# Swapping the two halves of the memory projection, and where the residual's norm runs

## The reference, cut to what matters

```python
x = x + mix @ w_out[l]

h = rms_norm(x, norm_x[l])            # "n2" in the kernel
m = rms_norm(mem, norm_mem[l])        # "nm", 256 tokens
q = (h @ xq[l]).reshape(B, S, XATTN_HEADS, XATTN_DH)
k, v = jnp.split(m @ xkv[l], 2, axis=-1)
...
q = rms_norm(q, xq_gain[l])
k = rms_norm(k, xk_gain[l])
s = jnp.einsum('bshd,bmhd->bhsm', q, k).astype(jnp.float32) * (XATTN_DH ** -0.5)
p = jax.nn.softmax(s, axis=-1).astype(v.dtype)
o = jnp.einsum('bhsm,bmhd->bshd', p, v).reshape(B, S, D)
x = x + o @ xo[l]
```

## Time and profile before

| | |
|---|---|
| median of 3 runs | 2663.01 us (2656.39 to 2664.89) |
| the profiled execution | 2657.79 us |
| its span in the trace | 2656.0 us |
| TensorE busy | 2451.6 us, 92% |
| VectorE, ScalarE, GpSimd busy | 989.9, 861.7, 841.8 us |
| mean granted clock of TensorE | 0.964 |

### The profile page before, as it was taken

The page is one execution under the profiler, slowest core; times in us unless marked ns, Lnnn a source line. Parts: engine busy times, 40 slices in busy tenths (PEclk is TensorE's granted clock), DMA queues, the critical chain, the costliest instruction groups (busy, mean ns, idle before and its releaser), DMA issues.

```text
span 2656.0 us, 33639 instructions
## 1 busy us (share of the span) xinstructions
PE 2451.6 (92%) x12246; PEld 1970.2 (74%) x12246; DVE 989.9 (37%) x1483; ACT 861.7 (32%) x1215; POOL 841.8 (32%) x347
## 2 busy tenths in 40 slices
PE   6989988887999997999999996999989998999997
PEld 4767567665878775888888883977766876678885
DVE  3231443148978787121111126034214443421114
ACT  3233344343422225221211223145433533432222
POOL 2222125303444443332222232232222023344442
PEclk9999789998999998999999998999999999999998
DMA  4112023223555552122221221222222012123322
GB/s 137 63 55 79 17 64 112 90 78 125 190 191 190 179 184 68 56 66 64 63 64 56 63 79 46 64 70 92 64 69 71 1 48 79 63 95 95 96 94 94
DMA packets 66563, 230.72 MB, mean 87 GB/s; under 512 B 7216, under 2 KB 9520, under 8 KB 66352
## 3 DMA queue, kind: packets, MB, share of 16 engines
q1 hardware_dynamic: 50224, 179.36, 21.1%
q10 hardware_dynamic: 16256, 50.21, 5.8%
HBM read 226.66 MB, written 2.10 MB: 86 GB/s over the span
## 4 chain that ended last, share of the span: by engine, by line
PE 50%; issue 37%; POOL 8%; DVE 4%; ACT 1%; DMA 1%; POOLq 0%; DVEq 0%; ACTq 0%; SPq 0%
PE ps L1258 35%; PE ps L1276 12%; POOL WLO L287 7%; DVE TN L1062 1%; DVE DOT L966 1%; PE ps L1470 1%; DVE TN L782 0%; DMA RAW<-in_stream_dram 0%; PE ps L1451 0%; PE ps L1317 0%; DMA CB<-in_c_dram 0%; PE ps L1360 0%; PE ps L1291 0%; ACT SQ L346 0%; DVE X L860 0%
## 5 line engine op out<-in xcount | busy, mean ns | idle before, releaser
L287 POOL TENSOR_TENSOR WLO<-RAW,WHI 128x1024 fp32r<-128x1024 f32 x335 | 829.6, 2481 | 1770.5 <-ACT WHI L314 1770.4
L314 ACT ACTIVATE WHI<-RAW 128x1024 fp32r<-128x1024 f32 x335 | 354.8, 1059 | 862.3 <-DMA RAW<-in_stream_dram 763.1
L1258 PE MATMUL ps<-HLO,WHI 128*128 128x512 f32 (+1 forms) x1312 | 438.6, 369 | 18.2 <-DVE OLO L835 5.2
L1258 PE MATMUL ps<-HHI,WLO 128*128 128x512 f32 (+1 forms) x1312 | 430.8, 363 | 1.9 <-issue 1.9
L1258 PE MATMUL ps<-HHI,WHI 128*128 128x512 f32 (+1 forms) x1312 | 430.6, 363 | 0.0
L1258 PEld LDWEIGHTS ps<-HLO,WHI 128*128 128x128 f32 x1312 | 227.9, 189 | 67.2 <-issue 25.2
L1276 PE MATMUL ps<-HHI,WHI 128*128 128x512 f32 (+1 forms) x640 | 223.4, 382 | 42.5 <-DVE HLO L1040 17.5
L1258 PEld LDWEIGHTS ps<-HHI,WHI 128*128 128x128 f32 x1312 | 227.9, 189 | 41.6 <-issue 2.9
L1258 PEld LDWEIGHTS ps<-HHI,WLO 128*128 128x128 f32 x1312 | 228.0, 189 | 39.3
L1258 PE MATMUL ps<-GLO,WHI 128*128 128x512 f32 x704 | 229.4, 366 | 16.8 <-DVE GLO L989 8.4
L984 DVE TENSOR_TENSOR SF<-SF,ps 128x512 f32<-128x512 f32 (+1 forms) x66 | 51.2, 777 | 490.4 <-PE ps L1258 368.5
(11 more groups left out here) (289 smaller groups left out, 3312.7 us busy)
## 6 DMA issues: line engine op xcount, KB each, us to landing
RAW<-in_stream_dram SPq DMA_DIRECT2D x335, 512.0 KB, 3.6
ADA<-in_ada_dram ACTq DMA_DIRECT2D x72, 512.0 KB, 3.9
BM<-in_bias_dram ACTq DMA_DIRECT2D x8, 448.0 KB, 3.8
DECAY<-in_decay_dram ACTq DMA_DIRECT2D x4, 512.0 KB, 3.7
out_dram<-X SPq DMA_DIRECT2D x8, 256.0 KB, 2.0
X<-in_x_dram SPq DMA_DIRECT2D x2, 512.0 KB, 5.8
X<-in_x_dram ACTq DMA_DIRECT2D x2, 512.0 KB, 7.6
C<-in_mem_dram ACTq DMA_DIRECT2D x1, 1024.0 KB, 5.4
```

The source lines that it names most:

```text
L287: nc.gpsimd.tensor_tensor(WLO[:, slot(u)], RAW[:, slot(u)], WHI[:, slot(u)].bitcast(F32), ALU.subtract).then_inc(unit_lo, 1)
L314: nc.scalar.activation(WHI[:, j], RAW[:, j], ACT.Copy).then_inc(unit_hi, 1)
L1258: mm = nc.tensor.matmul(out, w, x[:, k, tok], start=(k == 0 and n == 0), stop=(k == kt - 1 and n == 2))
```

## The change

The values come before the keys: in the stream of weights, on TensorE, on ScalarE and on VectorE. "n2" moves ahead of the keys on ScalarE and VectorE. Its sum over partitions stands on TensorE behind the first pair of values. On TensorE the wait for all eight residual tiles becomes a wait for the tile whose bank a pair of values takes. The converts inside "n2" are shifted by one: unit `xv`+3 is converted ahead of the norm, then one unit behind each of the first seven roundings. TensorE's wait for `xv` now stands ahead of the keys and its wait for `xk_q` ahead of the queries.

```diff
-... ("w_out", 8), ("xk", 8), ("xv", 8), ("xq", 8),
+... ("w_out", 8), ("xv", 8), ("xk", 8), ("xq", 8),
...
             act.wait_ge(*norm_at("n2", "acc", KD + 1))
+            convert(UNIT["xv"] + AHEAD)
+            norm("n2", None, KD, S, D, RS, SQ, TN, dst=HHI,
+                 between=lambda k: convert(UNIT["xv"] + AHEAD + k + 1) if k < 7 else None)
             normed("xk", UNIT["xk"], 2, 2, M, 256, SQ, RS)
-            act.wait_ge(s("xk_q"), 8)
-            norm("n2", None, KD, S, D, RS, SQ, TN, dst=HHI, between=lambda k: convert(UNIT["xv"] + AHEAD + k))
             normed("xq", UNIT["xq"], 2, 2, S, 256, SQ, RS)
...
-            normed("xk", UNIT["xk"], 2, 2, M, RS, ...)
             dve.wait_ge(s("w_out_x"), KD + 4)
             dve.wait_ge(*norm_at("nm", "lo", KD))
             norm("n2", lambda k: X[:, k], KD, S, lambda k: col("norm_x", k), RS, TN, HHI, HLO)
             for a in range(4):
                 wait_unit(UNIT["xv"] + 2 * a + 1)
                 V.tensor_copy(XV[:, :, 256 * a:256 * a + 256], ...).then_inc(s("xv"), 1)
+            normed("xk", UNIT["xk"], 2, 2, M, RS, ...)
...
-            pe.wait_ge(s("w_out_x"), KD + 4)
-            normed("xk", UNIT["xk"], 2, 2, M, const[:, ONES], SQ, (HHI, HLO), slice(S, N2))
-            sum_of("n2", TN[:, 1])
-            pe.wait_ge(s("xk_q"), 8)
             for a in range(4):
+                pe.wait_ge(s("w_out_x"), 4 + 5 + a)
                 unit_tokens([UNIT["xv"] + 2 * a, UNIT["xv"] + 2 * a + 1], 0, ...)
+                if a == 0:
+                    sum_of("n2", TN[:, 1])
             pe.wait_ge(s("xv"), 4)
-            pe.wait_ge(*norm_at("n2", "rs", 1))
+            normed("xk", UNIT["xk"], 2, 2, M, const[:, ONES], SQ, (HHI, HLO), slice(S, N2))
+            pe.wait_ge(s("xk_q"), 8)
             normed("xq", ...)
```

More of the change, by code:

```diff
@@ L50 @@
 MOD = 9 * KD
-_order = [("ret", 16), ("diff_qk", 8), ("diff_v", 4), ("w_out", 8), ("xk", 8), ("xv", 8), ("xq", 8),
+_order = [("ret", 16), ("diff_qk", 8), ("diff_v", 4), ("w_out", 8), ("xv", 8), ("xk", 8), ("xq", 8),
           ("xo", 8), ("ffn0", 3 * 22 + 2), ("ffn1", 68), ("na_q", 4), ("na_k", 4), ("na_v", 4),
@@ L926, in _ @@
             residual("w_out_x", UNIT["w_out"], also=lambda j, i: add_square("n2", TN[:, 1], SQ, j, 4 * i + j))
-            normed("xk", UNIT["xk"], 2, 2, M, RS, lambda i, j: XK[:, bass.ds(4 * i + j, 1)].rearrange("p o n -> p (o n)"),
-                   lambda j: col("xk_gain", j % 2))
             dve.wait_ge(s("w_out_x"), KD + 4)
@@ L935, in _ @@
                 V.tensor_copy(XV[:, :, 256 * a:256 * a + 256], ps[:, a].rearrange("p (c n) -> p c n", n=256)).then_inc(s("xv"), 1)
+            normed("xk", UNIT["xk"], 2, 2, M, RS, lambda i, j: XK[:, bass.ds(4 * i + j, 1)].rearrange("p o n -> p (o n)"),
+                   lambda j: col("xk_gain", j % 2))
             normed("xq", UNIT["xq"], 2, 2, S, RS, lambda i, j: XQ[:, bass.ds(4 * i + j, 1)].rearrange("p o n -> p (o n)"),
```

## The result

The changed kernel takes 2666.8 us (median of 10 runs, 2657.0 to 2671.4), the kernel before 2661.7 us (10 runs, 2656.4 to 2664.9). The ratio is 1.0023, with a 95% interval of 1.0013 to 1.0034: some 5 us slower by the medians and 6 by the ratio, within the 8 us that counted as no difference in the prediction, but on the slower side by the whole interval. The profiled execution took 2664.16 us with a span of 2662.4.

A forecast was written before the change was run, and what follows sets the result against it. TensorE, busy 92% of the span, was taken as the bound. Start -1.6, values +0.6, wait behind the values +3.0 and clock 0 made together +2 us on the median 2663.0, so 2665.0 us; range 2656 to 2672.

The forecast's parts named there:

- the gap moves from the queries to the keys and grows: The main case, given 80%: TensorE's wait for the values' copies grows by 3 us while the start gains 1.6.
- my bounds: Margins for the subtraction, the clock, the norm's chain and a later DMA: the difference could run from -1.3 to +7.7 us.
- The start: Between `w_out` and the values: the first matmul follows without the 1.37 us wait for the last residual tile, -1.6 us.
- The values: Values' stretch on TensorE: 30.0 us where it took 29.4, +0.6, with short waits for weights ahead of pairs 1 to 3.
- The wait behind the values: Ahead of the keys: last rounding follows a convert whose slot the last pair frees; 11.2 us against 8.18, +3.0.
- the last step, from the copies to TensorE: End of the wait ahead of the keys: TensorE starts 0.85 us after the last copy.
- The clock, and the wait ahead of the queries: Slow matmuls move from the queries' start to the keys'; queries follow a wait of about 1.3 us and are fast.
- the -1.5: At the queries' start: behind only a short wait the matmuls are fast and win back 1.5 us.
- the sum that I put at 0: Clock effects together: keys lose 1.5 us to slow matmuls, queries win back 1.5, net 0.
- The first: Ahead of the keys: the norm ends under the values, leaving a 1.5 us wait; -9.2, 2653.8 us; chance 6%.
- The second: In the values: roundings waiting for VectorE delay weights of pairs 2 and 3, 5.3 us late; +8.8, 2671.8 us; 10%.
- The tie that I named for pair 2: Norm's root ready at 416.0, DMA of pair 2's units landed at 415.8; taken as 0, up to 0.5 us.

The follow-up runs named there:

- experiment 5: Changed kernel with TensorE again waiting for all eight residual tiles ahead of the values; one trace, keys start at 42.9 us behind `w_out` instead of 41.2.
- Experiments 1: Changed kernel with the norm's last rounding on ScalarE put ahead of the convert of unit `xk`+2; ratio 1.0013 to the kernel before.
- 2: Changed kernel with the four copies of the values placed between the norm's steps on VectorE; ratios 0.9984 and, run again, 0.9981 to the kernel before.
- experiments 6: Changed kernel with three useless matmuls on TensorE ahead of the queries, before its wait for the keys' scaling; ratio 1.0029 to the kernel before.
- 8: Changed kernel with the values' copies between the norm's steps and three useless matmuls ahead of the queries; ratio 1.0005 to the kernel before.
- experiment 7: Changed kernel with one useless matmul, shaped like the norm's sum, ahead of the wait for the keys' scaling; one trace, 2667.3 us.
- experiment 9: Changed kernel with the values' copies between the norm's steps and one useless matmul ahead of the queries; ratio 0.9991 to the kernel before.

## Why the prediction was right, and where it was not

The time (2665.0 forecast, 2666.8 measured) and the class (no difference beyond 0.3%) were right, and so was the mechanism: the gap moves from the queries to the keys and grows. That the time is only 1.8 us off is in part luck: my base, the median of three runs, was 1.3 us above that of ten, and the difference that I forecast was +2 where 5 to 6 were measured, inside my bounds but well off the middle. By its steps:

- **The start.** The wait of 1.37 us went, as said; experiment 5 gives it 1.1.
- **The values.** Forecast 30.0 us, measured 30.5. The three waits were 1.47, 2.15 and 0.66, forecast 0.6, 2.6 and 0.5 to 1.9. The fourth unit's convert came at 410.71, not 409.95, and that is the excess ahead of pair 1.
- **The wait behind the values.** Forecast 11.2, measured 10.66. The chain of rows was right piece by piece: the rounding behind the convert, the subtraction at 2.43 where I took 2.47, the copies at 2.47. The only piece off was the last step, from the copies to TensorE, 0.43 instead of 0.85: I took the row of the queries for it, and by the rows of the next point those 0.85 go with the queries' start. Experiments 1 and 2 confirm the cause in two ways: with the last rounding freed the keys start 3 us sooner, with the copies moved 8.5.
- **The clock, and the wait ahead of the queries.** This is the step that failed. I wrote +1.5 for the keys and -1.5 for the queries, "they now follow a short wait like the 1.26". The keys did lose: against a fast trace their first 40 matmuls took 1.2 us more in the first trace of the changed kernel and 2.7 in the second. But the queries lost too, 2.8 and 2.0 us by the same count, where the kernel before lost 1.5. So the -1.5 came out as +1.3 and +0.5, and the sum that I put at 0 as 2.5 and 3.2 us. The wait ahead of the queries is 2.96 and not 1.3, for two reasons. I had written that the sum for the norm lay inside the keys' tail "and covered nothing"; without it the wait of 1.26 would have been 2.12 (it filled 437.73 to 438.59), and the change took it away. And what followed the keys before was the values, which started 0.05 us behind the last scaling; the queries start 0.89 behind it, much as they did behind the copies before (0.85):

```profile
438.92 0.88 DVE L847 SCALAR_TENSOR_TENSOR XK<-ps,vec,RS 128x256 f32 x2 [3.27 <-ACT RS L419]
479.88 0.88 DVE L848 SCALAR_TENSOR_TENSOR XK<-ps,vec,RS 128x256 f32 x2 [3.21 <-ACT RS L419]
```

(The first row is of the kernel before, where the values start at 439.85; the second of the changed kernel, where the queries start at 481.65.) With three useless matmuls in that place, in experiments 6 and 8, the queries were fast, at a granted clock of 1.00. Of the 3.4 us between my +2 and the 5.4 at the scores, the queries' clock is 2.8 and their later start 0.8; the other terms nearly cancel.

- **The rivals.** The first (the norm really lies under the values) didn't come about: VectorE's 28 us are under the values, but their end isn't. The second (the norm's steps hold up the weights) didn't either: in the changed kernel the convert of `xv`+6 waited 5.24 us for its DMA and that of the keys' first unit 6.77, so the roundings ahead of them had slack. The tie that I named for pair 2 stayed one: its first convert came at 415.85 behind a rounding, 3.8 us behind the end of pair 0.

About 1 us of the difference of the spans arose behind the scores and is not explained. In the other traces that rest is 2119 to 2128 us long, and the slow stretches of the clock fall differently in it each time; I didn't try to separate them. That spread of 9 us is larger than most differences in this document, and is why I read the stage in the traces and not only the times.

What stays open: why the queries were fast in 7 and slow in 9 with the same idle time ahead; why pair 1 of the values ran partly at the low clock in two of the fourteen traces (1 and 8, a granted clock of 0.77 over the pair in each), which delayed the last pair in both; and why the queries start 0.8 us later behind what releases them than the values do.

## What to carry to other kernels

Before moving a block to cover a wait, ask what the last instruction of that wait is tied to, and to what it is tied after the move. Here the work (the norm) was moved under other work, but its last step and the release of the banks stayed in one line behind the last transfer; four copies written between the steps, with nothing else changed, did what the reordering was meant to do; with the finer wait added, the old order comes within 0.6 us of the new one at the scores. Work that stands in a pause may not be free to move: behind 2.96 us of idle time the queries were slow here, and with three useless matmuls in that place they were fast and the scores came 2.8 us sooner. A pause of TensorE cost twice here, once as idle time (10.66 us ahead of the keys, 2.96 ahead of the queries) and once as slow matmuls behind it (1.2 and 2.8 us): count both, on every pause that the change lengthens.

## What the runs showed of the hardware that I had not expected

Six matmul rows (three float32 matmuls; the page then counts 12252 rows of TensorE and not 12246) added to TensorE's program where it is idle brought a wait of 6.65 to 6.8 us of "issue" some 440 us later, at the start of another loop, with transfers of instructions in or just before it, in all three kernels that had them. The other eleven traces wait 1.3 to 2.5 us there, for a residual tile, and at most 1.9 us of "issue" inside the loop. A gain of 2.8 us at one place was lost in this way at another. Counted from the scores, the three kernels reached the 80th matmul of that loop at 403.6 to 404.7 us, the kernel before at 400.1 and none of the other traces later than 402.3: a difference in time here did not have to arise near the edit.

A pause of 1.9 us ahead of the queries was followed by fast matmuls once (experiment 7, 1.94 us idle, then a granted clock of 1.00) and by slow ones once (experiment 9, 1.95 us idle, then 0.50 from the sixth matmul on). Two traces of the same changed kernel differ too, with 1.2 and 2.7 us lost at the start of the keys behind waits of 10.66 and 10.54. What sets the number of slow matmuls behind a pause is not shown.
